# First attention: values as the stationary operand, probabilities divided before the transposes, maxima from the mask's instruction

## The chip, the cores and the metric

The kernel runs on one core of a Trainium2 chip. The metric is the device time of one execution in microseconds (us). Three runs of the kernel before took 2552.7, 2553.87 and 2554.27 us; the median is 2553.87.

The engines are called TensorE (PE in the profile, with PEld for its loads of stationary operands), VectorE (DVE), ScalarE (ACT), GpSimd (POOL) and SyncE (SP, which issues the DMAs of the weights). Each has its own queue and works through it in order; they meet at semaphores.

## The reference, cut to what matters

Two transformer blocks on 256 positions of width 2048, all in float32. The change is in the two attentions.

```python
# first block: 16 heads of 64; each query sees its 64 best keys by an index score
rel = relu(einsum("bqhd,bsd->bqhs", q_idx, k_idx))
score = einsum("bqhs,bqh->bqs", rel, w_idx) * idx_scale      # causal by chunks of 64
_, sel = top_k(score, 64)
logits = einsum("bqhd,bqkhd->bqhk", q, k[sel]) * 64 ** -0.5
out = einsum("bqhk,bqkhd->bqhd", softmax(logits), v[sel])
# second block: 8 heads, two softmaxes each, with a bias by distance
logits = einsum('bqhcd,bkhcd->bhcqk', q, k) * 64 ** -0.5 + bias   # causal
p = softmax(logits)
w = p[:, :, 0] - lam * p[:, :, 1]
out = einsum('bhqk,bkhe->bqhe', w, v)
```

Around them stand the projections (weights of 2048 columns and more), a convolution of width 31 in the first block and one of width 3 in the second, and two gated feed-forward layers. The selection is computed as a mask over all 256 keys (0 for a selected key, -1e30 for another), so that no key is gathered.

## The kernel before

**The big matmuls.** All weights stream from memory in tiles of 1 MB. Each tile is cut into two pieces of 128 by 1024. ScalarE rounds a piece to the fast float format (`whi`), VectorE forms the rest (`wlo` = weight less `whi`), and TensorE multiplies three times: high by high (`whi,HTh`), high by the activations' rest (`whi,HTl`), low by high (`wlo,HTh`). A piece is three passes of four matmuls with 512 moving columns. There are 882 pieces, and this is nearly all of TensorE's time.

**Slots.** The program of each engine is a loop over the pieces; one turn is a slot. In slot s TensorE multiplies piece s, ScalarE rounds piece s + 3 and VectorE forms the rest of piece s + 3. Up to four pieces are in flight (four buffers `whi`, `wlo`), so that an engine can be some slots ahead of or behind another. All smaller work hangs in front of the slots as generators in a `Lane`: a job begins at a given slot, and `yield n` means "go on n slots later". In slots from 80 on, the jobs of a slot stand ahead of the slot's own piece on each of the three engines. What a slot holds is thus fixed when the program is built; when it happens is up to the semaphores.

**The first attention** (`attend`, one generator in each of the three engines' programs) works on two query blocks of 128 (t = 0 with 128 keys, t = 1 with 256) and on four groups g of four heads. Block 1 begins at slot 99, block 0 at slot 104; a group takes nine slots, so a period of nine slots holds one group of each block. The steps of a group, with their slots counted from its start:

- slot 0, TensorE: logits of four heads (L904), heads in turn from partitions 0 to 63 and 64 to 127. VectorE: scale and mask, four instructions (`stt` in the source, recorded under L1652, `SS<-bank,MK`), then the negated maxima of all four heads by one reduction (L1844).
- slot 2, ScalarE: the exponential with the maximum as its bias and the sum as a by-product (L1267).
- slot 3, TensorE: transposes of the probabilities (L911), after the last exponential. ScalarE copies them to SBUF (`stg`). VectorE: reciprocal of the sums (L1847).
- slot 5, TensorE: probabilities (stationary, 128 columns) times values (64 moving columns), L921; the output has queries on partitions.
- slot 5, VectorE: division of the output by the sums (L1853).
- slot 7, TensorE: two transposes of the output (recorded under L707, `bank<-ident,stg`), since the next matmul wants heads on partitions. ScalarE and VectorE split it into `ATh` and `ATl` (L1857).

The convolution's products on ScalarE (`PR`, L1092) and their sums on VectorE (`cv`, L1880 and L1652), and some long products for the modulation (`ada`, L1669, 2048 elements each with a sum), run in the same slots. Before the attention stands the selection (slots 84 to 98), which is work of VectorE above all.

**The second attention** (`differ`) has the same steps up to the exponentials; there the division came before the transposes already (`w1`), and the product with the values (L1032) has 128 moving columns, as its heads are 128 wide.

## Time and profile before

| | |
|---|---|
| median of three runs | 2553.87 us |
| the profiled execution | 2557.45 us, of which 2555.6 us are the span |
| TensorE busy | 2520.4 us, 99% of the span |
| VectorE busy | 1856.3 us, 73% |
| ScalarE busy | 1257.4 us, 49% |
| chain of work that ended last | TensorE 93%, VectorE 3%, DMA 2% |
| first attention | about 328 to 460 us |
| second attention | about 1545 to 1700 us |

The span runs from the first to the last instruction of one profiled execution; the time of the execution is a little longer. The shares are means over stages that differ: VectorE is near its limit in the first fifth of the span and half idle later. A matmul of the record overlaps the next one, so the time from the start of one group of matmuls to the start of the next is a better measure than its length. In the rows, "x4" merges four neighbours into one row with the time from the first's start to the last's end; a float32 matmul that is not in the fast format makes two records (four logits: x8).

### The profile page before, as it was taken

Reading aid. Unit: us, or ns where it says so; the run is one execution under the profiler, and the core shown is the slowest. Engines: PE = TensorE matmul, PEld = TensorE weight load, DVE = VectorE, ACT = ScalarE, POOL = GpSimd, SP = SyncE. Lnnn points to the kernel's source line nnn. Section 1 sums busy time; section 2 is a strip of 40 time slices with the busy share of each in tenths; the row PEclk is TensorE's granted clock in tenths of the full one; section 3 lists DMA queues with packets and bytes.
Section 4 is the critical chain, followed back from the end, with each engine's and each line's share of the span. In section 5 each row is a group of like instructions: output and inputs, shape, how many; then the busy total and the mean of one; then the engine's idle time right before and its main releaser. Section 6 shows DMA issues by size and latency. Waiting matters only on the chain.

```text
span 2555.6 us, 30085 instructions
## 1 busy us (share of the span) xinstructions
PE 2520.4 (99%) x11400; PEld 2073.7 (81%) x11400; DVE 1856.3 (73%) x2335; ACT 1257.4 (49%) x1731; POOL 3.9 (0%) x11
## 2 busy tenths in 40 slices
PE   7999999999999999999999999999999999999998
PEld 6787878888878888888888788888888888888886
DVE  8999999999877677557766667665666674456665
ACT  4434767764564444444444545554544444444443
POOL 0000000000000000000000000000000000000000
PEclk9999999999999999999999999999999999999999
DMA  9998656888946666666655554445455555555553
GB/s 383 355 349 307 227 208 220 291 289 314 363 179 234 225 213 233 245 231 214 216 213 198 182 203 175 161 178 200 177 191 197 192 203 198 197 192 189 196 198 116
DMA packets 80787, 578.23 MB, mean 226 GB/s; under 512 B 9166, under 2 KB 9462, under 8 KB 10881
## 3 DMA queue, kind: packets, MB, share of 16 engines
q1 hardware_dynamic: 79056, 567.25, 61.2%
q10 hardware_dynamic: 1074, 6.37, 0.6%
q0 software_dynamic: 512, 2.69, 0.3%
q8 instruction: 90, 1.47, 0.2%
q14 instruction: 55, 0.45, 0.0%
HBM read 574.15 MB, written 3.70 MB: 226 GB/s over the span
## 4 chain that ended last, share of the span: by engine, by line
PE 93%; DVE 3%; DMA 2%; ACT 1%; issue 1%; SPq 0%; DVEq 0%; ACTq 0%
PE bank L768 89%; DMA raw<-in_w_in 2%; DVE wlo L1659 1%; DMA aside<-in_w_in 1%; PE bank L707 1%; DVE raw L1669 0%; PE bank L921 0%; ACT whi L1092 0%; PE bank L969 0%; PE bank L883 0%; PE bank L1012 0%; DVE SC L1824 0%; DVE X L1652 0%; PE bank L1032 0%; PE bank L904 0%
## 5 line engine op out<-in xcount | busy, mean ns | idle before, releaser
L1659 DVE TENSOR_TENSOR wlo<-raw,whi 128x1024 fp32r<-128x1024 f32 x878 | 1062.8, 1222 | 561.5 <-ACT whi L1092 557.2
L1092 ACT ACTIVATE whi<-raw 128x1024 fp32r<-128x1024 f32 x878 | 917.0, 1058 | 912.1 <-PE bank L768 749.8
L768 PE MATMUL bank<-whi,HTh 128*128 128x512 f32 x2560 | 699.0, 394 | 11.1 <-ACT HTh L1092 4.6
L768 PE MATMUL bank<-wlo,HTh 128*128 128x512 f32 x2560 | 687.3, 390 | 1.6 <-DVE wlo L1659 1.6
L768 PE MATMUL bank<-whi,HTl 128*128 128x512 f32 x2560 | 687.8, 390 | 0.0
L768 PEld LDWEIGHTS bank<-whi,HTh 128*128 128x128 f32 x2560 | 474.4, 188 | 113.0 <-issue 10.5
L768 PEld LDWEIGHTS bank<-wlo,HTh 128*128 128x128 f32 x2560 | 481.2, 188 | 103.5 <-DVE wlo L1659 2.5
L768 PEld LDWEIGHTS bank<-whi,HTl 128*128 128x128 f32 x2560 | 481.7, 188 | 101.6
L1669 DVE CUSTOM_DVE_ANT_0 raw<-raw,GT,VECS 128x2048 f32<-128x2048 f32 x95 | 222.7, 2346 | 2.2 <-DMA raw<-in_w_ada 1.7
L768 PE MATMUL bank<-wlo,ACTh 128*128 128x512 f32 x704 | 188.8, 389 | 0.0
L768 PE MATMUL bank<-whi,ACTh 128*128 128x512 f32 x704 | 188.8, 389 | 0.0
L768 PE MATMUL bank<-whi,ACTl 128*128 128x512 f32 x704 | 188.8, 389 | 0.0
L2137 DVE STREAM_TRANSPOSE FT<-SG 32x256 f32<-32x256 f32 x352 | 153.2, 435 | 10.3
L768 PEld LDWEIGHTS bank<-whi,ACTh 128*128 128x128 f32 x704 | 132.1, 188 | 27.4
L768 PEld LDWEIGHTS bank<-whi,ACTl 128*128 128x128 f32 x704 | 132.1, 188 | 27.4
L768 PEld LDWEIGHTS bank<-wlo,ACTh 128*128 128x128 f32 x704 | 132.1, 188 | 27.4
L1092 ACT ACTIVATE PR<-uT,VECS 128x256 f32<-128x256 f32 x184 | 78.3, 501 | 15.9 <-DVE cv L1880 15.9
L1880 DVE TENSOR_TENSOR cv<-cv,PR 128x1024 f32<-128x1024 f32 x46 | 55.9, 1215 | 0.0
L768 PE MATMUL bank<-whi,CTh 128*128 128x512 f32 x128 | 35.2, 394 | 0.0
L768 PE MATMUL bank<-whi,ATh 128*128 128x512 f32 x128 | 35.0, 395 | 0.0
L768 PE MATMUL bank<-whi,CTl 128*128 128x512 f32 x128 | 34.6, 389 | 0.0
L768 PE MATMUL bank<-wlo,CTh 128*128 128x512 f32 x128 | 34.6, 389 | 0.0
(243 smaller groups left out, 1186.1 us busy)
## 6 DMA issues: line engine op xcount, KB each, us to landing
raw<-in_w_in SPq DMA_DIRECT2D x126, 1024.0 KB, 5.0
raw<-in_w_ada SPq DMA_DIRECT2D x95, 1024.0 KB, 6.4
raw<-in_w_gate SPq DMA_DIRECT2D x88, 1024.0 KB, 4.8
raw<-in_w_up SPq DMA_DIRECT2D x88, 1024.0 KB, 4.8
raw<-in_w_down SPq DMA_DIRECT2D x88, 1024.0 KB, 4.8
raw<-in_w_o SPq DMA_DIRECT2D x16, 1024.0 KB, 7.4
raw<-in_w_out SPq DMA_DIRECT2D x16, 1024.0 KB, 4.8
raw<-in_w_attn_out SPq DMA_DIRECT2D x8, 1024.0 KB, 4.8
```

The costliest lines, as they stand in the source:

```text
L707: i = e.transpose(dst[:, r * 128:r * 128 + 128], src[:, r * 128:r * 128 + 128], ident[:, :])
L768: i = e.matmul(bank[2 * ch.st + t][:, :], (xl if ps == 1 else xh)[:, k, tk(t)], (lo if ps == 2 else hi)[:, j * 512:j * 512 + 512], start=c ...
L1092: return e.activation(dst, src, ACT.Copy, scale=scale)
L1659: e.tensor_tensor(lo, src, r32(hi), S_).then_inc(lo_done, 1)
L1669: e.tensor_tensor_reduce(src, src, CB[:, :], 1.0, vec("bada", which * 16 + c), M_, A_, out).then_inc(ada_done, 1)
L1880: e.tensor_tensor(cv[:, h4, :], cv[:, h4, :], PR[hf][:, :, :], A_).then_inc(*cv_dve.one(j, hf, 0))
L2137: e.transpose(dst, src).then_inc(*f_turn[n].one(part, c, i))
```

## The change

In the first attention:

- The maximum is no longer a reduction of its own. The instruction that applies scale and mask also keeps the minimum of what it writes, which is now (logit + mask) times -0.125; the exponential is taken of minus that, head by head as they come.
- The reciprocal is followed at once by the division of the probabilities (128 x 4 x 128 or 256) in VectorE's slot 3, and the transposes wait for this division. They stand in slot 4 instead of 3.
- The product with the values has the values as the stationary operand (64 columns) and the transposed probabilities as the moving one (128 columns). Its output has heads on partitions: the even head of a pair on partitions 0 to 63, the odd one on 64 to 127, written by the two column halves of the array. It stands in slot 6 instead of 5.
- The output's division and transposes are gone; ScalarE's and VectorE's split of it stay in slot 7.

In the second attention only the maxima change in this way; the rows of the bias are multiplied by 8 once, when they are copied.

```diff
 # TensorE, attend(t)
-                yield 3
-                w.wait_ge(*att_act[t]("e3", g))
+                yield 4
+                w.wait_ge(*att_dve[t]("norm", g))
                 for p in R(t + 1):
                     for r in R(4):
                         i = e.transpose(bs[p][:, r * 128:r * 128 + 128], SS[t][:, r, p * 128:p * 128 + 128], ident[:, :])
...
-                for r in R(4):
-                    h = 4 * g + r
+                for two in R(2):
                     for p in R(t + 1):
                         sg = stg[[0, 1, 3][t + p]]
-                        i = e.matmul(bs[0][:, r * 64:r * 64 + 64], sg[:, r * 128:r * 128 + 128],
-                                     VV[:, p, h * 64:h * 64 + 64], start=p == 0, stop=p == t)
+                        for j in R(2):
+                            r = 2 * two + j
+                            h = 4 * g + r
+                            i = e.matmul(bs[0][64 * j:64 * j + 64, two * 128:two * 128 + 128], VV[:, p, h * 64:h * 64 + 64],
+                                         sg[:, r * 128:r * 128 + 128], start=p == 0, stop=p == t)
                 i.then_inc(*att_pe[t].one("PV", g))
-                yield 2
-                w.wait_ge(*att_dve[t]("norm", g))
-                transposes(bs[0], stg[2 + 2 * t], 2).then_inc(*att_pe[t].one("OT", g))
-                yield 2
+                yield 3
 # ScalarE, attend(t); the same first part in differ(t)
-                w.wait_ge(*att_dve[t]("max", g))
                 for r in R(4):
-                    e.activation(SS[t][:, r, 0:nk], SS[t][:, r, 0:nk], ACT.Exp, bias=att_mx[t][par][:, r:r + 1],
+                    w.wait_ge(*att_dve[t](f"l{r}", g))
+                    e.activation(SS[t][:, r, 0:nk], SS[t][:, r, 0:nk], ACT.Exp, bias=att_mx[t][par][:, r:r + 1], scale=-1.0,
                                  accum_out=att_sm[t][par][:, r:r + 1]).then_inc(*att_act[t].one(f"e{r}", g))
-                yield 1
+                yield 2
                 w.wait_ge(*att_pe[t]("TR", g))
...
-                yield 4
-                w.wait_ge(*att_pe[t]("OT", g))
+                yield 3
+                w.wait_ge(*att_pe[t]("PV", g))
 # VectorE, attend(t); the same first part in differ(t), with BT for MK
-                    stt(SS[t][:, r, 0:nk], src, 0.125, MK[:, t, 0:nk], M_, A_).then_inc(*ad.one(f"l{r}", g))
-                w.wait_ge(*ad("l3", g))
-                e.tensor_reduce(att_mx[t][par], SS[t][:, :, 0:nk], AX.X, ALU.max, negate=True).then_inc(*ad.one("max", g))
+                    e.tensor_tensor_reduce(SS[t][:, r, 0:nk], src, MK[:, t, 0:nk], -0.125, 3.0e38, A_, ALU.min,
+                                           att_mx[t][par][:, r:r + 1]).then_inc(*ad.one(f"l{r}", g))
                 yield 3
                 w.wait_ge(*att_act[t]("e3", g))
                 e.reciprocal(att_rc[t][par], att_sm[t][par]).then_inc(*ad.one("rec", g))
-                yield 2
-                w.wait_ge(*att_pe[t]("PV", g))
                 w.wait_ge(*ad("rec", g))
-                if g:
-                    w.wait_ge(*att_pe[t]("OT", g - 1))
-                e.tensor_tensor(tri(stg[2 + 2 * t][:, 0:256], 4), tri(bs[0][:, 0:256], 4),
-                                att_rc[t][par].unsqueeze(2).to_broadcast([128, 4, 64]), M_).then_inc(*ad.one("norm", g))
-                yield 2
+                e.tensor_tensor(SS[t][:, :, 0:nk], SS[t][:, :, 0:nk],
+                                att_rc[t][par].unsqueeze(2).to_broadcast([128, 4, nk]), M_).then_inc(*ad.one("norm", g))
+                yield 4
                 w.wait_ge(*att_act[t]("hi", g))
```

How the instructions stand, on TensorE first, from behind the logits of block 1's first group (slot 100) to the logits of block 0 (slot 104); a line with a plus is new at its place, one with a minus is gone from it. `SS_55` holds the probabilities of block 1.

```order
+L768 MATMUL bank<-whi,HTh 128x512 x4
+L768 MATMUL bank<-whi,HTl 128x512 x4
+L768 MATMUL bank<-wlo,HTh 128x512 x4
 L911 MATMUL bank<-ident,SS_55 128x128 x8
 L768 MATMUL bank<-whi,HTh 128x512 x4
 L768 MATMUL bank<-whi,HTl 128x512 x4
 L768 MATMUL bank<-wlo,HTh 128x512 x4
-L768 MATMUL bank<-whi,HTh 128x512 x4
-L768 MATMUL bank<-whi,HTl 128x512 x4
-L768 MATMUL bank<-wlo,HTh 128x512 x4
 L904 MATMUL bank<-kT,qT 128x128 x4
```

The transposes moved behind one more piece: four pieces stand between logits and transposes now, and one less between the transposes and block 0's logits.

On TensorE again, block 0's product with the values and what follows, up to the next group's transposes of block 1. Before (`stg_86` holds block 0's transposed probabilities, `stg_88` its divided output):

```order
L921 MATMUL bank<-VV,stg_86 128x64 x4
L768 MATMUL bank<-whi,HTh 128x512 x4
L768 MATMUL bank<-whi,HTl 128x512 x4
L768 MATMUL bank<-wlo,HTh 128x512 x4
L768 MATMUL bank<-whi,HTh 128x512 x4
L768 MATMUL bank<-whi,HTl 128x512 x4
L768 MATMUL bank<-wlo,HTh 128x512 x4
L707 MATMUL bank<-ident,stg_88 128x128 x2
L911 MATMUL bank<-ident,SS_55 128x128 x8
```

And of the change:

```order
L923 MATMUL bank<-stg_86,VV 64x128 x4
L768 MATMUL bank<-whi,HTh 128x512 x4
L768 MATMUL bank<-whi,HTl 128x512 x4
L768 MATMUL bank<-wlo,HTh 128x512 x4
L768 MATMUL bank<-whi,HTh 128x512 x4
L768 MATMUL bank<-whi,HTl 128x512 x4
L768 MATMUL bank<-wlo,HTh 128x512 x4
L911 MATMUL bank<-ident,SS_55 128x128 x8
```

The output's transposes are gone from their place, and the product writes 64 partitions by 128 columns.

On VectorE, block 1's first group from the mask (slot 99) to what follows the reciprocal (slot 102). Before:

```order
L1652 SCALAR_TENSOR_TENSOR SS_55<-bank,MK 128x256 x4
L1844 TENSOR_REDUCE STT<-SS_55 128x4
L1880 TENSOR_TENSOR cv<-cv,PR_74 128x1024
L1659 TENSOR_TENSOR wlo<-raw,whi 128x1024
L1652 SCALAR_TENSOR_TENSOR cv<-uT,VECS,cv 128x256 x4
L1659 TENSOR_TENSOR wlo<-raw,whi 128x1024
L1669 ISA raw,GTC<-raw,GT,VECS 128x2048
L1669 ISA GTC 128x1
L1659 TENSOR_TENSOR wlo<-raw,whi 128x1024
L1847 RECIPROCAL STT<-STT 128x4
L1652 SCALAR_TENSOR_TENSOR cv<-uT,VECS,cv 128x256 x4
```

And of the change, from the last of the four mask instructions on (each is now the instruction and a read-out of its minimum; the line numbers are those of the changed kernel):

```order
L1841 ISA SS_55,STT<-bank,MK 128x256
L1841 ISA STT 128x1
L1874 TENSOR_TENSOR cv<-cv,PR_74 128x1024
L1658 TENSOR_TENSOR wlo<-raw,whi 128x1024
L1651 SCALAR_TENSOR_TENSOR cv<-uT,VECS,cv 128x256 x4
L1658 TENSOR_TENSOR wlo<-raw,whi 128x1024
L1668 ISA raw,GTC<-raw,GT,VECS 128x2048
L1668 ISA GTC 128x1
L1658 TENSOR_TENSOR wlo<-raw,whi 128x1024
L1845 RECIPROCAL STT<-STT 128x4
L1847 TENSOR_TENSOR SS_55<-SS_55,STT 128x1024
L1651 SCALAR_TENSOR_TENSOR cv<-uT,VECS,cv 128x256 x4
```

The reduction left slot 99, and the division of the probabilities came in behind the reciprocal; what lies between them is the same.

## Rows read from the trace of the kernel before

**Rows 1.** Windows: busy us and instructions of PE, PEld, DVE, ACT, POOL; clock; DMA.
```profile
345.31:376.55 31.24, 31.24 (x165) 25.58 (x164) 30.57 (x44) 25.16 (x56) 0.00 (x0) 1.00 0.70 249
...
1580.00:1600.00 20.00, 20.00 (x103) 16.47 (x102) 13.98 (x24) 10.99 (x25) 0.00 (x0) 1.00 0.55 192
```

**Rows 2.** Timeline of PE, first group: start, length, line, out<-in, count [idle before].
```profile
337.06 1.07 PE L768 MATMUL bank<-wlo,HTh 128*128 128x512 f32 x4
338.81 1.09 PE L911 MATMUL bank<-ident,SS 128*128 128x128 f32 x8 [0.68 <-ACT SS L1267]
...
342.50 1.07 PE L768 MATMUL bank<-whi,HTh 128*128 128x512 f32 x4
...
345.31 0.71 PE L904 MATMUL bank<-kT,qT 64*128 64x128 f32 x8
345.96 2.00 PE L921 MATMUL bank<-VV,stg 128*128 128x64 f32 x16
347.76 1.18 PE L768 MATMUL bank<-whi,HTh 128*128 128x512 f32 x4
```

**Rows 3.** Timeline of PE, the rest of a period: outputs, transposes, logits, values.
```profile
353.34 0.38 PE L707 MATMUL bank<-ident,stg 128*128 128x128 f32 x2
353.48 1.17 PE L768 MATMUL bank<-whi,HTh 128*128 128x512 f32 x4
...
356.31 0.60 PE L911 MATMUL bank<-ident,SS 128*128 128x128 f32 x4
...
359.58 1.14 PE L904 MATMUL bank<-kT,qT 64*128 64x256 f32 x8
360.64 1.20 PE L768 MATMUL bank<-whi,HTh 128*128 128x512 f32 x4
...
363.50 1.00 PE L921 MATMUL bank<-VV,stg 128*128 128x64 f32 x8
364.30 1.18 PE L768 MATMUL bank<-whi,HTh 128*128 128x512 f32 x4
...
369.88 0.38 PE L707 MATMUL bank<-ident,stg 128*128 128x128 f32 x2
370.09 1.04 PE L911 MATMUL bank<-ident,SS 128*128 128x128 f32 x8
```

**Rows 4.** Timeline of VectorE (DVE), first group: mask, maxima, the reciprocals.
```profile
333.97 1.41 DVE L1652 SCALAR_TENSOR_TENSOR SS<-bank,MK 128x256 f32<-128x256 f32 x4
335.42 1.22 DVE L1844 TENSOR_REDUCE STT<-SS 128x4 f32<-128x1024 f32 x1
...
344.95 0.17 DVE L1847 RECIPROCAL STT<-STT 128x4 f32<-128x4 f32 x1
...
360.23 0.17 DVE L1847 RECIPROCAL STT<-STT 128x4 f32<-128x4 f32 x1
...
374.44 0.17 DVE L1847 RECIPROCAL STT<-STT 128x4 f32<-128x4 f32 x1
```

**Rows 5.** Timeline of PE, second attention: four products with values, what follows.
```profile
1566.88 1.16 PE L1032 MATMUL bank<-VV,stg 128*128 128x128 f32 x8
1567.80 1.17 PE L768 MATMUL bank<-whi,HTh 128*128 128x512 f32 x4
```

**Rows 6.** Timeline of VectorE: the instruction that also reduces, at 512 elements.
```profile
661.47 0.69 DVE L1953 CUSTOM_DVE_ANT_0 PR<-X,FO 128x512 f32<-128x512 f32 x1 [0.17 <-DVE STT L1953]
```

**Rows 7.** Timeline of PE at the start: the two longest stops.
```profile
13.97 3.75 PE L830 MATMUL bank<-stg,X 128*128 128x128 f32 x16 [4.37 <-ACT stg L1576]
22.31 2.05 PE L768 MATMUL bank<-whi,HTh 128*128 128x512 f32 x4 [4.59 <-ACT HTh L1092]
```

**Rows 8.** Windows around these stops (the granted clock is the number behind POOL).
```profile
14.00:16.00 2.00, 2.00 (x9) 2.00 (x10) 1.88 (x3) 0.11 (x1) 0.00 (x0) 1.00 1.03 430
...
21.00:22.00 1.00, 0.00 (x0) 0.00 (x0) 0.53 (x2) 1.00 (x2) 0.00 (x0) 0.55 0.98 410
...
27.00:28.00 1.00, 1.00 (x5) 0.81 (x5) 1.00 (x3) 0.00 (x0) 0.00 (x0) 0.54 1.01 418
```

More of the change, by code:

```diff
@@ L436, in build @@
                      + [(k, r) for r in R(8) for k in ("max", "out")] + ["mask"]) for t in R(2)]
-    att_pe = [steps(f"att{t}_pe", [(k, g) for g in R(4) for k in ("L", "TR", "PV", "OT")]) for t in R(2)]
+    att_pe = [steps(f"att{t}_pe", [(k, g) for g in R(4) for k in ("L", "TR", "PV")]) for t in R(2)]
     att_act = [steps(f"att{t}_act", [(k, g) for g in R(4) for k in
@@ L440, in build @@
     att_dve = [steps(f"att{t}_dve", [(k, g) for g in R(4) for k in
-                                     ("l0", "l1", "l2", "l3", "max", "rec", "norm", "lo")]) for t in R(2)]
+                                     ("l0", "l1", "l2", "l3", "rec", "norm", "lo")]) for t in R(2)]
     TAPS = [(j, hf) for j in R(KW) for hf in R(2)]
@@ L496, in build @@
     dif_dve = [steps(f"dif{t}_dve", [(k, g) for g in R(4) for k in
-                                     ("l0", "l1", "l2", "l3", "max", "rec", "lm0", "a0", "w0", "lm1", "a1", "w1")]
+                                     ("l0", "l1", "l2", "l3", "rec", "lm0", "a0", "w0", "lm1", "a1", "w1")]
                      + ["mean", "inv", "norm", "ev0", "lo0", "ev1", "lo1"]) for t in R(2)]
@@ L1153, in evict @@
                         for u in R(2):
-                            w.wait_ge(*att_pe[u]("OT", 3))
+                            w.wait_ge(*att_pe[u]("PV", 3))
                     square(stg[i % 6][:, :], B[:, :], SUMS[:, 8 * n + 4 * t + ch.j:8 * n + 4 * t + ch.j + 1]).then_inc(
@@ L1224, in bias_rows @@
             w.wait_ge(*rb_pe("rows"))
-            copy(RD[0:8, :], bank[5][0:8, 0:384]).then_inc(*rb_act.one("rows"))
+            copy(RD[0:8, :], bank[5][0:8, 0:384], 8.0).then_inc(*rb_act.one("rows"))
             yield 1
@@ L1517, in differ @@
                 yield 2
-                w.wait_ge(*dif_dve[t]("max", g))
                 for r in R(4):
-                    e.activation(SS[t][:, r, 0:nk], SS[t][:, r, 0:nk], ACT.Exp, bias=att_mx[t][par][:, r:r + 1],
+                    w.wait_ge(*dif_dve[t](f"l{r}", g))
+                    e.activation(SS[t][:, r, 0:nk], SS[t][:, r, 0:nk], ACT.Exp, bias=att_mx[t][par][:, r:r + 1], scale=-1.0,
                                  accum_out=att_sm[t][par][:, r:r + 1]).then_inc(*dif_act[t].one(f"e{r}", g))
@@ L2168, in differ @@
                     src = b[f"L{r % 2}"][:, r // 2 * 256:r // 2 * 256 + nk]
-                    stt(SS[t][:, r, 0:nk], src, 0.125, BT[:, 2 * g + r // 2, k0:k0 + nk], M_, A_).then_inc(
-                        *dd.one(f"l{r}", g))
-                w.wait_ge(*dd("l3", g))
-                e.tensor_reduce(att_mx[t][par], SS[t][:, :, 0:nk], AX.X, ALU.max, negate=True).then_inc(*dd.one("max", g))
+                    e.tensor_tensor_reduce(SS[t][:, r, 0:nk], src, BT[:, 2 * g + r // 2, k0:k0 + nk], -0.125, 3.0e38, A_,
+                                           ALU.min, att_mx[t][par][:, r:r + 1]).then_inc(*dd.one(f"l{r}", g))
                 yield 3
```

## The prediction

> **What bounds the kernel now.** I read the page first: TensorE is busy 99% of the span and makes up 93% of the chain of waits, so time is won or lost only where TensorE gets less to do or is left waiting. Then I read the stretch of the first attention by windows. One period of it (nine slots, one group of four heads for both query blocks) takes 31.24 us; TensorE is busy throughout, but VectorE has 30.57 us of work in it as well [rows 1]. Two engines are full here, and the change moves work on both. In the second attention VectorE has only 13.98 us of work in 20 and TensorE never waits [rows 1], so what the change saves there on VectorE (the reduction of the maxima, about 7 us) I cost at nothing for the end.
>
> Third, I laid TensorE's timeline beside VectorE's, slot by slot. The row to find on each is the same slot number. Query block 1 starts at slot 99; its transposes stand at the head of slot 102, at 338.81, its reciprocal at the head of VectorE's slot 102, at 344.95 [rows 2, 4]. So VectorE runs more than two slots behind TensorE at the start of attention. Until now that did no harm: the transposes waited for ScalarE's exponentials alone (0.84 us at 338, from 337.06 + 0.91 to 338.81), and the division came only after the product with the values.
>
> **The change part by part, on TensorE.** A plain slot takes 2.73 us and one behind a small group 2.83 to 2.85: two of them fill 347.76 to 353.34, one 353.48 to 356.31 [rows 2, 3]. So re-entering the big matmuls costs 0.11 us after each small group, and ahead of logits 0.08 more are lost (342.50 to 345.31 is 2.81).
>
> Removed: the transposes of the output, 0.14 us for block 1 (353.34 to 353.48) and 0.21 for block 0 (369.88 to 370.09) [rows 3]. The small groups stood at six places of a period and now stand at five (block 0's transposes share a place with block 1's logits): 0.11 less. I take off 0.07 as my estimate, as the logits now have to start right behind transposes. Together 0.39 us a period.
>
> Changed: the products with the values. Before: 1.80 us for eight (345.96 to 347.76) and 0.80 for four (363.50 to 364.30) [rows 2, 3]. They now have 64 columns of weights and 128 moving columns, and two heads go to the two column halves of the array. No row shows column halves. Row halves are shown by the logits, which alternate between partitions 0 and 64: four of 128 columns take 0.65 us (345.31 to 345.96), four of 256 take 1.06 (359.58 to 360.64), thus 0.24 fixed and 0.41 for each four of 128 [rows 2, 3]. Taken over to column halves, eight products cost 1.06 and four 0.65, plus 0.08 twice: 1.87 instead of 2.60, 0.73 saved. The other bound is the second attention's product, 128 by 128 on the whole array, one after another: four in 0.92 us (1566.88 to 1567.80), 0.23 each [rows 5]. With that, eight cost 1.84 and four 0.92, plus 0.24 + 0.08 twice: 3.40, 0.80 lost. I take the value of the logits, the nearest row: same type, same moving length, halves of the array.
>
> The Trainium skill, "TensorEngine Tiling (Array Packing)", section "Key Properties", says that tiles of the array run independently of each other, but that a change of the tiling mode drains the engine first. The logits' rows agree with both (the overlap, and the gap of 0.08 us); for column halves no row shows it. By this rule of the Trainium skill the sum would stay as chosen; by the row of the whole array it would rise by 6.1 us over four periods.
>
> So TensorE saves 0.39 + 0.73 = 1.1 us a period, 4.4 over four.
>
> **On VectorE and at the new wait.** The four mask instructions of a block had 0.36 us each and the maxima one reduction of 1024 elements (333.97 to 335.42, then 1.22 less an overlap of 0.08) [rows 4]. The instruction that also keeps a minimum is not shown at 256 elements from PSUM. At 512 from SBUF its row has 0.69 us [rows 6], 0.62 less the usual overlap, and 256 fewer elements (0.27, a quarter of the 1.14 of 1024 less a little fixed time) leave 0.35, the same as now. As an upper bound it costs the whole 0.62; below 0.35 I see nothing, since it goes over the same elements. I take 0.36. The reduction thus goes for 1.14 us in block 1 and 0.60 in block 0. The old division (256 elements, about 0.33 by the same rate) goes, the new one comes over the probabilities: 1.14 and 0.60. A period of VectorE loses 2.4 and gains 1.74.
>
> But now the transposes wait for the division. They stand one slot later, at the head of slot 103. TensorE reaches it at 337.97 + 2.73 = 340.7, as it no longer stops at 338. VectorE reaches the reciprocal at 344.95 - 1.14 = 343.8 and ends the division about 0.1 + 1.2 later, at 345.1. Behind the waiting transposes stand the weights' matmuls of slot 103 and everything after; nothing else can use TensorE. So a wait of **4.4 us appears and 0.84 goes: +3.6 us**. ScalarE's copies of the transposed block now wait there too, with one split of weights behind them, which is not due for two slots.
>
> Is it paid again? After the wait the two engines stand level. VectorE went from reciprocal to reciprocal in 374.44 - 344.95 = 29.5 us [rows 4]; less 0.66 that is 28.8, against TensorE's 30.1. So the distance opens by about 1.3 us a period. For block 0, VectorE's reciprocal at 360.23 moves to about 359.3 (less two reductions and an old division, plus a new one), up to 0.9 later if it waits for ScalarE's late split, and its division ends by 360.9 at the latest; the transposes come with block 1's logits, now at 359.58 [rows 3, 4], then at about 362. No second wait, with about 1 us to spare.
>
> **Sum.** +3.6 - 4.4 = -0.8 us. The profiled execution took 2557.45 us (span 2555.6 and 1.85 around it), so 2556.7 in its terms; the median of the three runs is 3.6 lower, at 2553.87, and the forecast in its terms is **2553.1**. A measurement of this kernel tells about 0.2%, 5.1 us, from no change; the forecast is no change.
>
> **Rivals.**
>
> *The clock falls in the wait.* Early in this trace TensorE stood still for 4.37 us and then for 4.59 us. Behind the first it had 1.00 (2.4 GHz), in the second the granted clock fell to the lower level, 0.5 (1.2 GHz), between 21 and 22 us, and came back only near the end of 27 to 28 us [rows 7, 8]. From 22.31 to about 27.9 it did half its work: 2.8 us lost. For it: my wait of 4.4 lies between the two. Against it: TensorE was only lightly used before both, and is full before mine. Time: 2553.1 + 2.8 = 2555.9. The Trainium skill, "TensorE: Matmul & The Clock Gate", section "HAM oscillation — how this bites in real kernels", holds that waits in mid-kernel send the engine back to its low clock and that the ramp is paid again each time; of the two idle stretches here one agrees and one does not.
>
> *Slower: the column halves take turns.* If the two heads' products run one after the other, four periods lose 0.41 each (0.80 - 0.39) and the wait still costs 3.6: +5.2, 2559.1. For it: no row shows them side by side, and every product loads new weights. Against it: the logits do so too and overlap. It decides from 0.23 us for each product, against 0.13 to 0.16 in pairs.
>
> *VectorE limits every group.* If the new instruction costs 0.62 us at any length, block 1 pays 1.0 more and block 0 about 1.5 (its four of 128 elements cost 0.9 now, by the rate above); VectorE's period becomes 31.4 against 30.1 and the wait returns three more times at 1.3, and the first grows by 1.0: -0.8 + 1.0 + 3.9 = +4.1, 2558.0. It decides from 0.17 us more for each of the eight. Against it: the fit to 512 and to the plain instruction.
>
> *No wait at all, faster.* If VectorE is in time for slot 103, 4.4 and the old 0.84 are both saved: 2548.6. For it would speak a VectorE that is ahead; the rows show it behind by two slots when the first group is still young, and the work ahead of the attention is left as it was.
>
> **Chances.** Forecast 0.46, clock 0.22, halves in turn 0.14, VectorE 0.11, no wait 0.07. Slower by over 0.2% are the halves in turn, most of the time, and a few mixed cases: 0.10. Faster by over 0.2% only the case without a wait, in most of its spread: 0.05. Within: 0.85. The likeliest case alone spans 2551.3 to 2555 (0.7 for the instruction's price, about 1 for the products, and the runs' own 1.5). The range takes in the clock and most of the VectorE case and leaves out both ends: 2551.0 to 2558.5.
>
> **What would show it.** In the first attention: one idle stretch of TensorE of 4 to 5 us near 341 to 345, ended by VectorE's write of the probabilities, and none like it later; logits of block 0 near 349 instead of 345.31; periods of about 30.1 us; the products with values at about 1.1 and 0.65 us; no transposes of the output; the new instruction near 0.36 us; clock 1.00 all through. Products of about 1.8 us, a clock of 0.5 behind the wait, or a second wait at the next groups show the rivals. A wait under 2 us, or none, would make the step on VectorE's lag wrong.

## The result and the profile after

The changed kernel takes 2558.99 us (median of 18 runs, 2556.84 to 2559.78); the kernel before, on the same chips, 2553.26 us (18 runs, 2551.39 to 2555.35). The ratio is 1.0020, with a 95% interval of 1.0014 to 1.0026: the change costs 3.6 to 6.6 us, and 5.7 by the medians. The forecast was 2553.1 us, with 2551.0 to 2558.5 as its range: 5.9 us too low, and half a microsecond too low at the range's upper end.

The spans of the two profiled executions (2555.6 and 2556.0 us) hide this. The one of before lost some 4 us ahead of the first attention, whose logits begin at 328.60 there and between 323.3 and 326.6 in all other profiled executions of this study; its trace shows TensorE idle for 1.94 us at 215.38 (0.31 at the same place in the changed kernel), with a granted clock of 0.50 behind it. So I compare from the first logits to the convolution's sums, the next fixed point behind the attention; TensorE's timeline has both. Before:

```profile
328.60 1.14 PE L904 MATMUL bank<-kT,qT 64*128 64x256 f32 x8
...
530.66 3.61 PE L933 MATMUL bank<-cv,ones 128*128 128x256 f32 x16
```

That is 202.06 us. After, TensorE's timeline of the first period (answers to [rows 2, 3]):

```profile
324.44 1.13 PE L904 MATMUL bank<-kT,qT 64*128 64x256 f32 x8
...
335.63 1.07 PE L768 MATMUL bank<-wlo,HTh 128*128 128x512 f32 x4
341.08 1.34 PE L911 MATMUL bank<-ident,SS 128*128 128x128 f32 x8 [4.38 <-DVE SS L1847]
342.08 2.06 PE L768 MATMUL bank<-whi,HTh 128*128 128x512 f32 x4
...
346.47 0.72 PE L904 MATMUL bank<-kT,qT 64*128 64x128 f32 x8
...
350.06 1.09 PE L923 MATMUL bank<-stg,VV 128*64 128x128 f32 x16
351.08 1.20 PE L768 MATMUL bank<-whi,HTh 128*128 128x512 f32 x4
...
361.77 0.70 PE L911 MATMUL bank<-ident,SS 128*128 128x128 f32 x4 [2.24 <-DVE SS L1847]
362.40 2.08 PE L904 MATMUL bank<-kT,qT 64*128 64x256 f32 x8
364.41 1.76 PE L768 MATMUL bank<-whi,HTh 128*128 128x512 f32 x4
...
370.65 0.66 PE L923 MATMUL bank<-stg,VV 128*64 128x128 f32 x8
371.24 1.21 PE L768 MATMUL bank<-whi,HTh 128*128 128x512 f32 x4
...
531.13 3.61 PE L932 MATMUL bank<-cv,ones 128*128 128x256 f32 x16
```

From 324.44 to 531.13 are 206.69 us, 4.63 more than before. From there to the end both take 2024.9 us, so the new maxima in the second attention cost and gain nothing, as forecast. There are two stops for the division, not one, and the matmuls behind both take up to twice their time: logits that took 1.06 us [rows 3] take 2.01 (362.40 to 364.41). The windows around the stops show why; the granted clock is the number behind POOL, as in [rows 8]:

```profile
340.00:341.00 1.00, 0.00 (x0) 0.00 (x0) 1.00 (x2) 0.00 (x0) 0.00 (x0) 1.00 1.05 418
...
342.00:345.00 3.00, 3.00 (x9) 2.42 (x9) 2.88 (x4) 2.54 (x6) 0.00 (x0) 0.50 0.45 153
...
346.00:348.00 2.00, 2.00 (x15) 1.39 (x14) 1.81 (x8) 2.00 (x6) 0.00 (x0) 1.00 0.96 406
...
363.00:365.00 2.00, 2.00 (x9) 1.17 (x6) 1.46 (x4) 2.00 (x6) 0.00 (x0) 0.50 0.96 406
...
366.00:368.00 2.00, 2.00 (x10) 1.66 (x9) 2.00 (x2) 0.79 (x1) 0.00 (x0) 1.00 0.00 0
```

After each stop TensorE works at 0.50 (1.2 GHz) for some 3 us. Later periods are what was hoped for: no stop, 30.09 us instead of 31.24. The same windows as [rows 1]:

```profile
394.01:424.10 30.09, 30.09 (x162) 23.77 (x161) 29.32 (x49) 23.62 (x52) 0.00 (x0) 1.00 0.65 231
1580.00:1600.00 20.00, 20.00 (x103) 16.49 (x102) 12.54 (x26) 11.03 (x24) 0.00 (x0) 1.00 0.53 186
```

VectorE's timeline answers to [rows 4]. The first two rows are the new instruction for two neighbouring heads; over the four heads it costs 0.345 us from start to start. The third row is block 1's new division, the last is block 0's:

```profile
329.82 0.42 DVE L1841 CUSTOM_DVE_ANT_0 SS<-bank,MK 128x256 f32<-128x256 f32 x1
...
330.16 0.42 DVE L1841 CUSTOM_DVE_ANT_0 SS<-bank,MK 128x256 f32<-128x256 f32 x1
...
339.80 1.22 DVE L1847 TENSOR_TENSOR SS<-SS,STT 128x1024 f32<-128x1024 f32 x1
...
357.05 0.42 DVE L1851 TENSOR_TENSOR ATl<-bank,ATh 128x256 fp32r<-128x256 f32 x1 [1.98 <-ACT ATh L1091]
359.68 1.23 DVE L1658 TENSOR_TENSOR wlo<-raw,whi 128x1024 fp32r<-128x1024 f32 x1 [2.20 <-ACT whi L1091]
360.82 0.18 DVE L1845 RECIPROCAL STT<-STT 128x4 f32<-128x4 f32 x1
361.03 0.69 DVE L1847 TENSOR_TENSOR SS<-SS,STT 128x512 f32<-128x512 f32 x1
```

Ahead of block 0's division VectorE itself stands idle, for ScalarE. And ScalarE's timeline shows for whom ScalarE waits:

```profile
354.13 1.09 ACT L1139 ACTIVATE X<-bank 128x512 f32<-128x512 f32 x2 [3.73 <-PE bank L768]
355.10 0.40 ACT L1266 ACTIVATE SS<-SS,STT 128x128 f32<-128x128 f32 x1
...
356.91 1.71 ACT L1091 ACTIVATE PR<-uT,VECS 128x256 f32<-128x256 f32 x4
358.52 1.06 ACT L1091 ACTIVATE whi<-raw 128x1024 fp32r<-128x1024 f32 x1
```

At 354.13 it empties a finished chunk's accumulators, which TensorE's own pass releases. Behind that in its queue stand block 0's exponentials, a convolution product and the split `whi`, then on VectorE `wlo`, reciprocal and division: 7.8 us from the pass that ends at 353.9 to the start of the transposes at 361.77. TensorE has only two slots of other work (5.4 us) between that pass and the transposes. The loop from TensorE over ScalarE and VectorE back to TensorE is longer than that by 2.4 us, and so TensorE stops.

### The profile page after: what moved, and what is told of

Read it like the earlier page. It is cut to its first block, busy times and chain, and to the rows that moved or that the text cites. A ratio compares the mean times of both kernels' runs of the same rounds, so it can differ in the third digit from the quotient of the medians.

```text
span 2556.0 us, 30090 instructions
## 1 busy us (share of the span) xinstructions
PE 2516.6 (98%) x11384; PEld 2067.3 (81%) x11384; DVE 1847.2 (72%) x2383; ACT 1257.8 (49%) x1731; POOL 3.9 (0%) x11
## 4 chain that ended last, share of the span: by engine, by line
PE 91%; DVE 5%; DMA 2%; ACT 1%; issue 1%; SPq 0%; DVEq 0%; ACTq 0%
PE bank L768 87%; DVE wlo L1658 2%; DMA raw<-in_w_in 2%; DVE raw L1668 1%; DMA aside<-in_w_in 1%; PE bank L707 1%; DVE PART L1741 0%; ACT whi L1091 0%; PE bank L968 0%; PE bank L883 0%; PE bank L1011 0%; PE bank L904 0%; PE bank L923 0%; DVE SC L1823 0%; DVE X L1651 0%
```

## The experiments

Two theories stand. A: TensorE's saving of 1.15 us a period is real, and is outweighed by the two stops and by the clock behind each. B: the saving is eaten where it is made (matmuls on column halves, the new instruction), or the stops are VectorE's shortage of time and only move. The medians are differences from before in the same runs. Their intervals reach some 2 us to either side, so several kernels can't be told from before, or from each other, by their medians alone; the readings below rest on the stretch and the stops, which come from one profiled execution of each. "Stretch" is the time from the first logits to the convolution's sums, less 202.06. The sum is -5.44 (4 x 1.15 and the old wait of 0.84), plus the stops' idle time, 0.15 for each stop (the old one showed 0.68 idle and cost 0.84), plus the loss by the clock (from the transposes to the next small group, passing over logits right behind them, against 3.72 us at the first stop and 7.32 at the second where the clock held). The column "clock" has this loss in us.

| kernel | median, us | ratio (95%) | stretch | stops for the division | clock | sum |
|---|---|---|---|---|---|---|
| changed | +5.7 | 1.0014 to 1.0026 | +4.63 | 4.38, 2.24 | 1.67, 1.56 | +4.71 |
| e1 two slots later | +3.8 | 1.0006 to 1.0024 | +3.52 | 0.54, 0.80, 0.80 (and 2.80 for ScalarE) | 1.60 | |
| e2 maxima only | -0.7 | 0.9989 to 1.0007 | -1.02 | none | 0 | |
| e3 block 0 earlier | +1.6 | 0.9997 to 1.0014 | +0.80 | 4.39 | 1.68 | +0.78 |
| e4 filled wait | +2.0 | 0.9999 to 1.0017 | +1.46 | 0.50, 2.22 | 0 | +1.62 |
| e6 division first | -1.3 | 0.9985 to 1.0002 | -1.07 | 2.70 | 1.59 | -1.00 |
| e5 both earlier | -3.0 | 0.9980 to 0.9998 | -2.88 | 1.21, 1.02 | 0 | -2.91 |
| e7 one slot | -0.7 | 0.9987 to 1.0005 | -1.98 | 0.94, 2.22 | 0 | -1.98 |
| e8 halves in turn | +0.3 | 0.9991 to 1.0008 | +0.39 | 2.23 | 1.50 | +0.40 |
| e9 conv later | +5.0 | 1.0012 to 1.0029 | +5.29 | five, 6.56 in all | 1.55 | |
| e10 all three | +2.4 | 1.0001 to 1.0019 | +2.06 | 1.69, 1.08, 1.68 | 0 | |
| e11 before, conv later | +3.8 | 1.0003 to 1.0022 | +3.19 | none (1.48 for the exponentials) | 0 | |
| e12 conv later still | +7.1 | 1.0017 to 1.0038 | +7.79 | five, 7.13 in all | 1.54 | |
| e13 exponentials only | +1.7 | 0.9999 to 1.0017 | +2.19 | 4.38, 0.69 | 2.27 | +2.20 |
| e14 division 0 only | +2.4 | 1.0002 to 1.0020 | +2.34 | 4.38, 1.48 | 1.66 | +2.38 |
| e15 division on ScalarE | -4.6 | 0.9975 to 0.9993 | -4.19 | 1.07 | 0 | -4.22 |

For e4 the sum holds 4.04 us for the added matmuls, for e8 4 x 0.49 for the slower products. Stops and clock losses are read from the same traces as the stretch, so the sum is an account and no forecast; it lies within 0.2 us of the measured stretch in all ten kernels for which it is made, which leaves little room for anything else. In the others (e1, e9 to e12) there are stops for ScalarE and for `wlo` too, and I have not accounted for each tenth.

**e2: only the maxima, transposes to outputs as before.**

```diff
 # before, VectorE; the exponentials then take scale=-1.0 and wait for each l{r}; the same in differ
-                    stt(SS[t][:, r, 0:nk], src, 0.125, MK[:, t, 0:nk], M_, A_).then_inc(*ad.one(f"l{r}", g))
-                e.tensor_reduce(att_mx[t][par], SS[t][:, :, 0:nk], AX.X, ALU.max, negate=True).then_inc(*ad.one("max", g))
+                    e.tensor_tensor_reduce(SS[t][:, r, 0:nk], src, MK[:, t, 0:nk], -0.125, 3.0e38, A_, ALU.min,
+                                           att_mx[t][par][:, r:r + 1]).then_inc(*ad.one(f"l{r}", g))
```

> The kernel before with the maxima alone changed, in both attentions; transposes, products with values and division as before. Theory A: TensorE's program is the same and VectorE only gains time, so the time is that of before within 1 us, and the reciprocal of the first group comes about 1.1 us earlier behind its logits. Rival (the instruction that keeps the minimum is dearer than 0.36 us, or delays the exponentials): TensorE waits more for the exponentials, 0.84 us grows, and the time rises by 1 us or more.

As theory A has it. The reciprocal stands 15.15 us behind the first logits (339.69 and 324.54) instead of 16.35 (344.95 [rows 4] and 328.60), 1.2 us earlier, and the first transposes no longer wait at all: 1.0 us of stretch. The instruction is not to blame.

**e1: TensorE's transposes two slots later.**

```diff
 # TensorE; the same two slots on ScalarE ahead of cp and on VectorE ahead of lo; block 0 begins two slots later
-                yield 4
+                yield 4 + 2 * (t == 1 and g == 0)
                 w.wait_ge(*att_dve[t]("norm", g))
```

> The changed kernel with the first transposes of block 1 two slots later, and everything that follows in the attention two slots later with them; the division stays where it is. Theory A (the waits of TensorE for the division, 4.4 and 2.2 us, and the lower clock behind each, about 1.6 us each, outweigh a real saving of TensorE of 1.1 us a period): no wait for the division above 0.5 us is left in the first attention, the granted clock stays at 1.00, periods of about 30.1 us, and the time is 4 to 5.5 us below before, about 10 below the changed kernel. Rival B (the matmuls on column halves or the new instruction cost as much as they save, the waits are made good later): the waits go, but the time stays within 2 us of the changed kernel's, some 4 above before.

The first stop went, and the gain did not come: rival B's number. ScalarE's and TensorE's timelines show where it went:

```profile
345.33 1.71 ACT L1091 ACTIVATE PR<-uT,VECS 128x256 f32<-128x256 f32 x4 [6.43 <-DVE cv L1874]
...
347.89 1.05 ACT L1091 ACTIVATE stg<-bank 128x512 f32<-128x512 f32 x2
```

```profile
348.99 0.71 PE L904 MATMUL bank<-kT,qT 64*128 64x128 f32 x8 [2.80 <-ACT stg L1091]
```

A convolution product on ScalarE waits for VectorE's late sums, the copies of the transposed block stand behind it in the queue, and block 0's logits wait for the bank that these free. VectorE's lateness was handed to TensorE by another way, with the clock's loss (1.60 us) behind it. A TensorE that waits less gets to the next thing that VectorE owes it.

**e4: the first wait filled with matmuls that nobody reads.**

```diff
+                if t == 1 and g == 0:
+                    for r in R(9):
+                        e.matmul(bank[7][:, 0:256], qT[:, 0, tk(1)], kT[:, 0, 0:256], start=True, stop=True)
                 w.wait_ge(*att_dve[t]("norm", g))
```

> The changed kernel with nine more matmuls of 256 columns on TensorE ahead of the first transposes (about 0.43 us each, 3.9 us in all), with a result that nobody reads, so that TensorE works through most of its first wait. If the wait's idle time lowers the clock: the granted clock stays at 1.00 behind the first transposes, these begin at the same distance from the first logits (16.6 us), the three passes behind them take 2.8 instead of 4.4 us, and the time is 1.5 to 2 us below the changed kernel, with the second wait and its loss still there. If the clock falls for another reason, or the lower clock costs nothing: no change within 0.7 us.

The transposes come at the same distance, 16.6 us behind the first logits (325.55), and now the clock stays (line numbers move by the edit):

```profile
337.63 4.04 PE L910 MATMUL bank<-kT,qT 128*128 128x256 f32 x18
342.18 1.09 PE L914 MATMUL bank<-ident,SS 128*128 128x128 f32 x8 [0.50 <-DVE SS L1850]
345.95 0.72 PE L904 MATMUL bank<-kT,qT 64*128 64x128 f32 x8
...
361.25 0.66 PE L914 MATMUL bank<-ident,SS 128*128 128x128 f32 x4 [2.22 <-DVE SS L1850]
361.83 1.13 PE L904 MATMUL bank<-kT,qT 64*128 64x256 f32 x8
```

So behind the first stop it is the idle time that lowers the clock: 3.77 us from transposes to logits instead of 5.39. The saving was larger than expected (3.2 us in the stretch), since behind the second stop, as long as in the changed kernel, the clock held too.

**e3, e13, e14: the second stop.** e3 moves block 0's exponentials and division one slot earlier, e13 the exponentials alone (ahead of the chunk's eviction), e14 the division alone (ahead of the waiting `wlo`), the last two in the first group only.

```diff
 # e13, ScalarE (and one slot more ahead of TR); e3: yield 1 + t in all groups
-                yield 2
+                yield 2 - (t == 0 and g == 0)
                 for r in R(4):
 # e14, VectorE (and one slot more ahead of lo); e3: yield 2 + t in all groups
-                yield 3
+                yield 3 - (t == 0 and g == 0)
                 w.wait_ge(*att_act[t]("e3", g))
```

> The changed kernel with block 0's exponentials and its reciprocal and division one slot earlier on ScalarE and VectorE, in all four groups; TensorE's order is the same. If the second wait (2.24 us at 361.8) comes from the exponentials standing behind the eviction of a chunk in ScalarE's queue, which waits for the delayed TensorE, it goes: the first wait of about 4.4 us stays with the lower clock behind it, the second is under 0.5 us and the clock stays at 1.00 there, and the time is 3 to 4 us below the changed kernel. If VectorE is simply late with its own work, a second wait of 1.5 us or more stays and the time moves by less than 1 us.

> The changed kernel with only block 0's exponentials of the first group one slot earlier on ScalarE, ahead of the eviction of a chunk instead of behind it; VectorE's order is the same. If the second wait is the length of the queue from that eviction (which TensorE's own pass releases) over four exponentials, two products and two splits on ScalarE to VectorE's split, reciprocal and division: it falls by the 1.55 us of the exponentials, from 2.24 to about 0.7, the clock stays at 1.00 there, and the time is 2.5 to 3.5 us below the changed kernel. If it is VectorE's own load: it stays at 2 us or more.

> The changed kernel with only block 0's first reciprocal and division one slot earlier on VectorE, ahead of the split that waits for ScalarE; ScalarE's order is the same. By the queue from the eviction the division then hangs on the exponentials alone and ends near 33.2 us after the first logits instead of 37.3, the second wait goes, and the time is 3 to 4 us below the changed kernel; the first wait stays. If it is VectorE's own load: a wait of 1 us or more stays.

In e3 the second stop is gone and the clock stays there. In e13 it shrinks by exactly the four exponentials, from 2.24 to 0.69:

```profile
360.66 0.66 PE L911 MATMUL bank<-ident,SS 128*128 128x128 f32 x4 [0.69 <-DVE SS L1847]
```

In e14 it is gone, but the next block 1 waits:

```profile
358.20 0.60 PE L911 MATMUL bank<-ident,SS 128*128 128x128 f32 x4
...
373.32 1.10 PE L911 MATMUL bank<-ident,SS 128*128 128x128 f32 x8 [1.48 <-DVE SS L1847]
```

So the second stop comes from the loop over the eviction. That it is a loop, and not an echo of the first stop, shows in its length: 2.22 to 2.24 us in the changed kernel, e4, e7, e9 and e12, whether the first stop was 4.38, 0.50, 0.94 or none. (The 2.23 of e8 is of another kind, as shown with e8 below.) In the later groups the eviction and block 0's exponentials fall into different slots (eight slots between chunks, nine between groups), and the stop is not there.

**e6, e7, e5: the first division earlier on VectorE**, by two slots (e6), by one (e7), and by two together with e3's edit (e5).

```diff
 # e6; e7 has - 1; e5: yield 2 + t - 2 * (t == 1 and g == 0), and e3's lines
-                yield 3
+                yield 3 - 2 * (t == 1 and g == 0)
                 w.wait_ge(*att_act[t]("e3", g))
```

> The changed kernel with one thing moved: for block 1's first group alone, reciprocal and division stand two slots earlier in VectorE's queue (slot 100 instead of 102, ahead of two splits of weights, a convolution sum and a long product for the modulation, about 6 us of work); TensorE's and ScalarE's orders are the same. Theory A (the wait is made by what stands ahead of the division on VectorE, and all that was lost follows from it): the division ends by about 335.5 on a scale on which the first logits start at 324.9, the first wait of 4.4 us, the second of 2.2 us and both losses of clock go; from the first logits to the convolution's sums 197 us, against 202.1 before and 206.7 in the changed kernel; the time is 4 to 5.5 us below before. Rival (VectorE's lag is only handed on, as in the run with TensorE two slots later: to the rest of the weights, to ScalarE's products or to block 0): another wait of 2 us or more appears within the next two groups, and the time is within 2 us of before.

> The changed kernel with the first division one slot earlier on VectorE instead of two (behind one of the two splits, ahead of the long product). The first wait should shrink from 4.4 to 0.9 to 1.5 us. If the loss of clock goes with the length of the wait, the clock stays at 1.00 behind it and the time is at most 1.5 us above the run with the division two slots earlier. If any wait at this place costs the clock, another 1.5 us is lost, and the second wait may come back.

> As the run with the division first, and block 0's exponentials, reciprocal and division one slot earlier too (in all groups). By theory A both waits go, 4 to 5.5 us below before, and nothing more than by moving the first division alone, as the second wait followed from the first. If the second wait has a cause of its own, this one is 2 us or more faster than the other. If VectorE's lag is only handed on: within 2 us of before.

In e6 the first stop is gone, as theory A had it, and the second is 2.70 us, as the rival had it: there VectorE works without a gap from 328.95 on and is late by its own load:

```profile
353.08 1.23 DVE L1658 TENSOR_TENSOR wlo<-raw,whi 128x1024 fp32r<-128x1024 f32 x1
354.22 0.17 DVE L1845 RECIPROCAL STT<-STT 128x4 f32<-128x4 f32 x1
```

This reciprocal comes 30.64 us behind the first logits (323.58). In e7 the first falls to 0.94 and the clock stays, through the second too:

```profile
338.46 1.09 PE L911 MATMUL bank<-ident,SS 128*128 128x128 f32 x8 [0.94 <-DVE SS L1847]
...
357.52 0.66 PE L911 MATMUL bank<-ident,SS 128*128 128x128 f32 x4 [2.22 <-DVE SS L1847]
358.11 1.14 PE L904 MATMUL bank<-kT,qT 64*128 64x256 f32 x8
```

With both (e5) two stops of 1.21 and 1.02 are left, the clock stays, and the kernel is faster than before. My expectation that e5 gains nothing over e6 was wrong: it gains 1.8 us of stretch, so the second stop does not follow from the first. The 4 to 5.5 us below before, expected of e6, came in neither.

**e9 to e12: less convolution ahead of the first group.**

```diff
-        return CONV0 + 4 * n // 3 if n < 11 else SEL0 + 12 + 32 * (n - 11) // 25
+        return CONV0 + 4 * n // 3 if n < 11 else SEL0 + 16 + 30 * (n - 11) // 25   # e9, e10 (on e5), e11 (on before)
+        return CONV0 + 4 * n // 3 if n < 11 else SEL0 + 20 + 28 * (n - 11) // 25   # e12
```

> The changed kernel with the convolution's taps from the twelfth on begun four slots later and packed a little closer (30 slots for 25 half taps instead of 32), so that they end in the same slot; attention as in the changed kernel. Some three half taps of 1.14 to 1.6 us, 3.4 to 4.7 us of work, leave VectorE's queue ahead of the first group. If all that the change loses is VectorE's lag at the start of the attention: the first wait falls from 4.4 to under 1 us, the second goes, the clock stays at 1.00, from the first logits to the convolution's sums about 197 us instead of 202.1 before, and the time is 4 to 5.5 us below before. If VectorE, now with about 0.9 us more a period, becomes the limit of the later periods: waits of 0.5 us or more for the division at groups three and four, and the time within 2 us of before.

> The later convolution together with the earlier divisions and exponentials of the run with both earlier. If VectorE's lag is all: no wait above 0.3 us in the first attention, 5 us below before and no more than 0.7 us below the run with the later convolution alone. If the later periods are VectorE's: the same waits there as in that run.

> The kernel before with the later convolution alone. If the convolution's place matters only through the wait for the division: within 1 us of before, as only the wait of 0.84 us for the exponentials can change. If the later place is a gain of its own: 2 us or more below before.

> The changed kernel with the convolution's taps begun eight slots later and packed into 28 slots. The first wait is gone as with four slots; VectorE gets about 1.5 us more in each later period and is level with TensorE's 30.1 there. If that is near its limit: waits of 0.5 us or more for the division at the third and fourth group, and 1 to 3 us above the run with four slots. If VectorE still has room: the same as that run.

A miss, and a useful one. The first stop goes in e9, e10 and e12, but the stop of 2.22 behind the eviction stays in e9 and e12, and with the packed convolution TensorE waits for VectorE in the later periods, at groups two to four (0.63, 1.26, 1.64, 0.81 in e9). Even the kernel before loses 3.8 us by it (e11; a stop of 1.48 for the exponentials appears at its second group). VectorE has hardly any room in this attention, in either kernel (30.57 us of work in 31.24 before [rows 1], 29.32 in 30.09 after); that this is the whole reason is not shown.

**e8: all even heads, then all odd heads** (on e6).

```diff
-                for two in R(2):
-                    for p in R(t + 1):
-                        sg = stg[[0, 1, 3][t + p]]
-                        for j in R(2):
+                for j in R(2):
+                    for two in R(2):
+                        for p in R(t + 1):
+                            sg = stg[[0, 1, 3][t + p]]
```

> As the run with the division first, with the products with values in another order: all of the even heads (one column half), then all of the odd heads (the other half), so that neighbours share a half. If two neighbours on different halves run side by side: eight products take 1.7 to 1.9 us instead of 1.0 and four take 1.0 instead of 0.6, a period grows by about 1.3 us and the time by about 5 us over the run with the division first. If the halves never overlapped, or overlap whatever the order: no change within 1 us.

```profile
343.44 1.58 PE L923 MATMUL bank<-stg,VV 128*64 128x128 f32 x16
344.95 1.19 PE L768 MATMUL bank<-whi,HTh 128*128 128x512 f32 x4
...
395.03 0.66 PE L923 MATMUL bank<-stg,VV 128*64 128x128 f32 x8
395.62 1.21 PE L768 MATMUL bank<-whi,HTh 128*128 128x512 f32 x4
```

Eight products take 1.51 us instead of 1.02, four take 0.59 as before. The total alone does not show the halves side by side, as the order also brings together the products that add into the same output, in the eight only. The starts of the single records settle it (a record does not name its half; the program's order does). In e6 they come in pairs 0.006 us apart, with a pair every 0.109 us once under way. In e8 the first four start one by one, 0.16 and then 0.109 us apart, all on one half; a second row of records at 0.109 us begins 0.49 us behind the first of all, runs beside the first row for eight records, and ends alone with four. So the halves do run side by side, adding into the same output costs nothing extra (0.109 us in both orders), and what is lost is the late start of the second half. The expected sizes were too large.

The stop of 2.23 in e8 is VectorE's own load, as in e6: VectorE has no gap ahead of its reciprocal (354.68), and TensorE comes 0.49 us later, which makes 2.2 of e6's 2.70.

**e15: on e5, the first division of block 1 by ScalarE.** With stops left only where VectorE is late, I took 1.14 us off it.

```diff
 # ScalarE, t == 1 and g == 0, a slot behind the exponentials; VectorE leaves out this one division
+                    w.wait_ge(*att_dve[t]("rec", g))
+                    for r in R(4):
+                        m = copy(SS[t][:, r, 0:nk], SS[t][:, r, 0:nk], att_rc[t][par][:, r:r + 1])
```

> The run with both earlier, with the first division of block 1 taken from VectorE (1.14 us) and done by ScalarE as four copies with a scale per query (about 0.42 us each), right behind the exponentials, where ScalarE stands idle. If the waits left in that run (1.21 and 1.02 us) are VectorE's load in the first two groups: both fall to 0.3 us or less, and the time is 1.5 to 2.5 us below it, about 5 below before. If they are something else: no change within 0.7 us, or a new wait of the first transposes for ScalarE.

```profile
333.21 1.71 ACT L1093 ACTIVATE SS<-SS,STT 128x256 f32<-128x256 f32 x4 [0.28 <-DVE STT L1855]
```

```profile
336.13 1.03 PE L913 MATMUL bank<-ident,SS 128*128 128x128 f32 x8
...
352.80 0.66 PE L913 MATMUL bank<-ident,SS 128*128 128x128 f32 x4
...
367.54 1.09 PE L913 MATMUL bank<-ident,SS 128*128 128x128 f32 x8 [1.07 <-DVE SS L1858]
```

The stop of 1.21 is gone; the other, 1.02 in e5, stayed at 1.07, against the expectation for it. At 2549.18 us against 2553.75 this kernel beats both, by 4.6 us against before and about 10 against the changed kernel: most of what TensorE saves is there once the divisions are in time.

## Why the prediction was wrong, step by step

**TensorE's saving: right.** 1.1 us a period was forecast, 1.15 came (31.24 [rows 1] to 30.09); the products take 1.02 and 0.59 us, forecast from the logits as 1.06 and 0.65. The rival of halves in turn is excluded by these times; in e8's order, where the halves overlap for a part only, the products cost 0.49 us a period more, about 2 us in all.

**The new instruction: right.** 0.345 us from start to start, forecast 0.36. The rival in which VectorE limits every group by its price is excluded by e2.

**The first wait: right, and not by luck.** 4.38 us, forecast 4.4, from two rows of two engines laid beside each other by slot numbers. Both terms came: the reciprocal stood 15.15 us behind the first logits (339.59 and 324.44), forecast 15.2 (343.8 and 328.60), and TensorE's stop began 12.3 us behind them, forecast 12.1.

**"No second wait, with about 1 us to spare": the step that failed.** It followed VectorE alone and allowed 0.9 us for a late split. The forecast has block 0's reciprocal 30.7 us behind the first logits (359.3 and 328.60); it came 36.38 behind (360.82 and 324.44). VectorE's own work was right: in e6, where it has no gap, the same reciprocal comes at 30.64. Between the two divisions VectorE waited 5.5 us for ScalarE (1.30 for an earlier split, and the 1.98 and 2.20 in the rows above), because in ScalarE's queue the exponentials and the split that VectorE needs stand behind the eviction, which waited 3.73 us for TensorE's own pass. In e9 and e12 it waits for that pass as well (3.73 and 3.21 us), without a first stop. I had seen ScalarE's copies wait and dismissed the split behind them as "not due for two slots"; the eviction and the exponentials, which the forecast does not name, were what counted. Cost: 2.24 us and 0.15, shown by e13 and e14.

**The clock: a rival that held.** It had a chance of 0.22 and a price of 2.8 us once; it came twice, at 1.67 and 1.56. The argument against it, that TensorE is full ahead of the wait, did not hold: TensorE was full and the clock fell, and e4 shows the first fall to be the idle time's. The Trainium skill, "TensorE: Matmul & The Clock Gate", section "HAM oscillation — how this bites in real kernels", holds that a long enough wait in mid-kernel sends the engine back to its low clock and that this is paid for each time. The stops of 2.70 us and more in this stretch agree, with one fall behind each; of six stops of 2.22 to 2.24 us two show none.

Together: -0.8 forecast, +4.6 measured in the stretch; between them lie 5.4 us, and the second stop (2.39) and the clock (3.23) make 5.6. I priced the cases apart, as rivals, and so had the sum of two outside the range.

## What to carry to other kernels

Where a step gets a new wait, lay all engines of the loop beside each other, not only the one waited for: a queue that is worked through in order can hold what the waiting engine needs behind something that waits for this engine itself, and the way round can be longer than the slots allowed for it (here 7.8 us against 5.4). Price the clock's fall with every idle stretch of the main engine as long as those that cost it in the trace, and add it to the wait rather than holding it as an alternative. A saving on a full engine comes in only as far as the next engine has room; here moving block 0's exponentials and divisions one slot and giving block 1's first division to an engine that stood idle (e15) took some 10 us off the changed kernel, against 4.6 that TensorE's four periods save.

## What the runs showed of the hardware

- *The clock and the length of a stop.* In this stretch, with TensorE full before, the granted clock held behind all stops up to 1.69 us, fell to 0.50 behind 2.70, 2.80 and four times 4.38 or 4.39, and did either behind six stops of 2.22 to 2.24: it fell in the changed kernel, e8, e9 and e12 and held in e4 and e7. Outside this stretch the lengths overlap further: in the trace of before it fell behind 1.94 us (at 215.38), and early in that trace it held behind 4.37 [rows 7, 8]. So the length alone does not decide, and what else does stays open. Each fall in this stretch cost 1.5 to 1.7 us, once 2.3 (e13).
- *Column halves.* With heads in turn, records on the two halves start 0.006 us apart (e6). With one half's products first (e8), four products cost the same as with heads in turn, 0.59 us, and eight cost 0.49 us more, as the second half's first record starts 0.49 us behind the first half's. The Trainium skill, "TensorEngine Tiling (Array Packing)", section "Key Properties", says that tiles can run in parallel. The pairs in e6 agree; the late start in e8 shows that this depends here on the order in which the products stand.
- *A stop costs more than its idle entry*, by about 0.15 us: with that the sums above close.
